# Down weights of expert 0 and up weights of expert 1 issued behind the load of the first expert's rows

## The reference

```
h = rms_norm(x)                                   # per token
group = argmax over 4 groups; top 2 of its 4 experts
a = h @ w1[e] ; b = h @ w3[e]                     # 16 experts, 1024 -> 256 each
hid = silu(a) * b * combine[e]
x = x + sum over the two experts of hid @ w2[e]   # 256 -> 1024
```

## Time and profile before

| | us |
|---|---|
| median of 3 runs | 1974.15 (1974.12 to 1975.18) |
| the profiled execution, its own time | 1973.74 |
| its span, first to last instruction | 1971.8 |
| matrix engine busy | 1899.3 (96%) |
| vector, scalar, GpSimd busy | 1134.3, 477.5, 400.4 |
| DMA moved | 376.32 MB, mean 191 GB/s |

### The profile page before, as it was taken

One profiled execution on the slowest core, in us unless ns is written; L12 is line 12 of the kernel. 1 busy time (PEld: TensorE's weight loads), 2 busy tenths in 40 slices (PEclk: granted clock), 3 DMA queues, 4 the chain that ended last, 5 costly groups with the idle time before them and its releaser, 6 DMA issues.

```text
span 1971.8 us, 25238 instructions
## 1 busy us (share of the span) xinstructions
PE 1899.3 (96%) x9028; PEld 1251.7 (63%) x9028; DVE 1134.3 (58%) x2171; ACT 477.5 (24%) x1048; POOL 400.4 (20%) x310
## 2 busy tenths in 40 slices
PE   8999999999999999999699999999999999999993
PEld 5655658755665545888565556586566655468882
DVE  4788732644786866111667886436457778641126
ACT  3133313343221011111132333132432300111112
POOL 1322233122220012000324222421222200210013
PEclk9999999999999999999899999999999999999997
DMA  4555677422328405999832121122223392179996
GB/s 178 203 203 203 228 276 270 176 99 79 127 86 322 156 33 217 411 393 369 329 112 113 75 75 75 43 86 81 86 86 118 126 347 91 70 274 424 384 373 235
DMA packets 77915, 376.32 MB, mean 191 GB/s; under 512 B 6705, under 2 KB 15281, under 8 KB 64578
## 3 DMA queue, kind: packets, MB, share of 16 engines
q1 hardware_dynamic: 43154, 260.35, 34.3%
q10 hardware_dynamic: 26000, 82.90, 11.0%
q0 software_dynamic: 8640, 31.46, 4.2%
HBM read 262.44 MB, written 113.30 MB: 191 GB/s over the span
## 4 chain that ended last, share of the span: by engine, by line
PE 89%; DVE 4%; DMA 3%; ACT 1%; issue 1%; POOL 1%; ACTq 0%; DVEq 0%; SPq 0%; POOLq 0%
PE bank L1030 41%; PE bank L2175 11%; PE bank L2035 8%; PE bank L2060 5%; PE bank L2210 5%; PE bank L1043 3%; PE bank L1056 2%; PE bank L1083 2%; PE bank L1121 2%; PE bank L742 2%; PE bank L1095 1%; PE bank L2167 1%; PE bank L1220 1%; PE bank L725 1%; DMA blocks<-ring,slots 1%
## 5 line engine op out<-in xcount | busy, mean ns | idle before, releaser
L1030 PE MATMUL bank<-x,ring 128*128 128x384 f32 x1056 | 360.2, 489 | 2.3 <-issue 2.3
L1030 PE MATMUL bank<-hT,ring 128*128 128x384 f32 x1056 | 359.7, 490 | 0.1
L1030 PEld LDWEIGHTS bank<-x,ring 128*128 128x128 f32 x1056 | 195.0, 190 | 135.2 <-issue 12.5
L1030 PEld LDWEIGHTS bank<-hT,ring 128*128 128x128 f32 x1056 | 195.3, 190 | 133.0 <-issue 10.2
L1525 DVE SCALAR_TENSOR_TENSOR reg_a<-cvx,pp,reg_a 128x783 f32<-128x783 f32 x120 | 142.7, 1189 | 4.3
L1284 ACT ACTIVATE sums<-bank 128x384 f32<-128x384 f32 x132 | 64.9, 491 | 250.0 <-PE bank L1030 243.9
L2571 DVE SCALAR_TENSOR_TENSOR prob<-prob,bank 128x256 f32<-128x256 f32 x30 | 12.6, 421 | 180.8 <-ACT prob L2290 180.7
L1468 DVE SCALAR_TENSOR_TENSOR gbuf<-bank,sums 128x384 f32<-128x384 f32 x96 | 53.5, 557 | 88.0 <-PE bank L1030 82.1
L1805 POOL TENSOR_TENSOR ring<-dg,ring 128x512 f32<-128x512 f32 x24 | 34.1, 1421 | 257.1 <-PE bank L1030 257.1
L2258 ACT ACTIVATE prob<-x 128x1024 f32<-128x1024 f32 x12 | 12.7, 1058 | 291.7 <-DVE x L2423 291.7
L2035 PE MATMUL bank<-oT,wide 128*128 128x384 f32 x256 | 82.9, 486 | 0.0
(11 more groups left out here) (387 smaller groups left out, 3276.2 us busy)
## 6 DMA issues: line engine op xcount, KB each, us to landing
ring<-in_wd SPq DMA_DIRECT2D x26, 2048.0 KB, 9.2
blocks<-hT SPq DMA_DIRECT2D x16, 3072.0 KB, 22.1
gate_dram<-gbuf ACTq DMA_DIRECT2D x64, 384.0 KB, 2.3
ring<-gate_dram SPq DMA_DIRECT2D x16, 1536.0 KB, 7.3
ring<-in_we SPq DMA_DIRECT2D x8, 2048.0 KB, 15.0
hT<-blocks ACTq DMA_DIRECT2D x26, 512.0 KB, 9.3
wide<-in_we SPq DMA_DIRECT2D x6, 2048.0 KB, 23.1
oT<-in_we SPq DMA_DIRECT2D x6, 2048.0 KB, 21.4
```

The lines of the kernel that those rows point to most:

```text
L1030: mm = nc.tensor.matmul(bank[i % 2][:, 0:HALF], w[:, k, :], a[:, k, :], start=(k == 0 and r in (0, 1, 3)), stop=(k == 3), skip_group_check ...
```

## The change

```
                 sp.wait_ge(out_mm, last_pair + 2)
                 load_up(sp, 0)
-                sp.wait_ge(out_mm, last_pair + 5)
-                load_down(sp, 0)
-                load_up(sp, 1)
                 sp.wait_ge(out_mm, last_pair + 6)
                 sp.wait_ge(scattered_first, 16 * TOP * FROM_BLOCKS * (layer + 1))
                 sp.dma_start(x_in[0], block_rows[0]).then_inc(block_in[0], 16)
+                load_down(sp, 0)
+                load_up(sp, 1)
                 sp.wait_ge(out_mm, last_pair + 7)
                 sp.wait_ge(scattered, 16 * TOP * (T - FROM_BLOCKS) * (layer + 1))
                 sp.wait_ge(block_in[1], 16)
```

## The result

| | before | changed |
|---|---|---|
| median of 9 runs, us | 1975.55 (1974.12 to 1977.14) | 1978.68 (1977.76 to 1982.62) |
| ratio, 95% interval | | 1.0018 (1.0009 to 1.0026) |
| span of the profiled execution, us | 1971.8 | 1976.5 |

A second timing of the changed kernel (`e4_after_again`, 11 runs) gave 1.0012 (1.0003 to 1.0021). So the change costs 0.12 to 0.18%, by these ratios 2.4 to 3.6 us. The change lies within the 0.2% that the prediction called no change, but it is measurable, and the predicted range (to 1978.0) does not reach the first median, 1978.68.

The account below looks back on a forecast made before the run. PE was taken as the bound, busy 1899.3 of 1971.8 us. Layer 0 -0.7 and layer 1 +1.6 gave +0.9 us, so 1974.6, plus 0.4 for the median: 1975.0; range 1971.4 to 1978.0.

Parts of the forecast that it names:

- the two weight loads held up the fourth tile's write: Ahead of the experts: SP's loads delayed GpSimd's write by 4.7 us in layer 0 and 3.7 us in layer 1.
- From the read to the end of the writes I had 17.8 us: Layer 0: block's read issued at 769.9, all tiles written (`scattered`) at 787.7, weights passing first, then the writes.
- In layer 1 I had +1.6 us: Layer 1: `scattered` at 1761.5 instead of 1759.89, so `turn_in(1)` at 1765.4 instead of 1763.74.
- the three signs that I had named for being wrong: ACT's rows issued before 786 or after 789.5; granted clock of 0.5 behind 791; PE waiting for expert 2's up weights.
- layer 0's term, -0.7 us: Layer 0: -0.2 us at `turn_in(1)` (791.3 against 791.51), and the 0.52 us wait for hidden values gone.
- With nothing of SP's in flight the write lands at 766.33 + 3.5.: Layer 0, fourth tile's write: landing at 769.85, 3.5 us as for the write at 746.67, instead of 8.2 us.
- the rows' own flight: Ahead of `turn_in(1)`: expert 1's rows take 3.56 us from ACT's issue, so PE can turn at 791.3.
- the collision itself: Tiles five and six: 3.15 MB of weights and 2.10 MB of writes pass together; `scattered` at 787.7, bounds 785.4 and 789.5.
- My own worst bound: All bytes at 324 GB/s, `scattered` at 789.5: layer 0 +1.0, layer 1 +3.4, together +4.4 us.
- the clock rival: Both layers: PE's idle 2.2 us ahead of `turn_in(1)` makes the clock fall, 1.7 us each; +4.3, 1978.4; chance 0.12.
- The rival "queues share": Tile five's writes go in between the weights, only tile six's are late; `scattered` near 785.5, time 1971.3; chance 0.16.
- its counter-evidence: Against sharing: from 764 to 768 GpSimd's queue had work (issued at 764.0 and 766.33) and moved nothing.

Follow-up runs that it names:

- e4_after_again: The changed kernel once more, unchanged, for a second profile and ratio; 1977.48 us, ratio to before 1.0012.
- e4: Short spelling of `e4_after_again`: the changed kernel once more, unchanged; 1977.48 us, ratio to before 1.0012.
- e8: The changed kernel with 34 (layer 0) and 17 (layer 1) idle transposes of the matrix engine ahead of `turn_in(1)`; ratio to before 1.0016.
- e2: Against the changed kernel: down weights of expert 0 back at their old place, up weights of expert 1 issued only when all tiles are written; 1981.81 us, 1.003.
- e3: Against the changed kernel: both moved weight loads issued only when all tiles are written; 1982.28 us, 1.0033.
- e6: The changed kernel's queue order and waits, with an eighth of the two moved loads' bytes (0.39 MB for 3.15 MB); 1971.22 us, 0.9978.
- e9: Against before: only the up weights of expert 1 (2 MB) moved behind the read of expert 0's block; 1971.24 us, 0.9978.
- before again: The kernel before, unchanged, for a second profile; its profiled execution took 1972.40 us.
- e1: Against before: only the down weights of expert 0 (1 MB) moved behind the read of expert 0's block; 1971.2 us, 0.9977.
- e7: Before with only the down weights of expert 0 (1 MB) moved behind the block's read, a repeat timing; 1971.9 us, 0.9978.

## Why the prediction was wrong

Right, by its own steps: the two weight loads held up the fourth tile's write; without them the block's read is issued 3.3 us (layer 0) and 3.7 us (layer 1) sooner; `turn_first` does not wait, and the one-hot matrix is next; the moved loads themselves are never late; the writes of tiles five and six pass behind the weights. From the read to the end of the writes I had 17.8 us; it was 17.9 and 17.6. In layer 1 I had +1.6 us, and it was +1.6, in part by luck: 1.3 at `turn_in(1)`, where 1.6 were forecast, and 0.3 behind it, where PE waits 0.44 us for expert 2's weights, which I had ruled out. Of the three signs that I had named for being wrong, two appeared, the granted clock at half behind 791 (0.52 from 794.1 to 797.4) and this wait; the third, rows issued after 789.5, appeared only on the profile's axis (789.65, or 789.25 without the 0.4 us by which the mark had moved).

Of the 3.7 us between the forecast 1975.0 and the median 1978.68, 1.4 are the base: I built on the first three runs of before (1974.15), and nine gave 1975.55. The rest is the change itself, +3.1 timed (+2.1 in `e4`) where I had +0.9; between the profiled executions the two layers show +4.3.

The step that failed is layer 0's term, -0.7 us; it measured +2.7. The 3.4 us are:
- **1.4 us, the write's landing.** "With nothing of SP's in flight the write lands at 766.33 + 3.5." In layer 0 it lands 4.9 us after its issue. The weights had held it up by 3.3 us (8.2 against 4.9), not by the 4.7 of the prediction. From the DMA issues of the changed kernel, that write in layer 0 and in layer 1:

```profile
blocks<-ring,slots POOLq DMA_INDIRECT x1, 4.9
...
blocks<-ring,slots POOLq DMA_INDIRECT x1, 3.5
```

and two queues of the same kernel from 765 to 770:

```profile
q0 software_dynamic: 278, 1.02, 50.8%
q8 instruction: 1, 0.02, 1.8%
```

A 16 KB packet of instructions (q8) passes there, and in layer 1 none does. One execution had it in layer 1 as well, `e8`, where the write took 5.4 us (its DMA from 1741 to 1746, and the issue at 1742):

```profile
q8 instruction: 1, 0.02, 2.3%
...
blocks<-ring,slots POOLq DMA_INDIRECT x1, 5.4
```

In the ten profiles of kernels with the read ahead of a moved load, this write took 4.9 to 5.4 us in the eleven places with such a packet, 3.5 in the seven without it and without SP's weights in flight, 4.2 in the two with weights. Both profiles of before had the packet in layer 0 too, and none in layer 1: the 8.2 against 7.2 us, which I had put down to the weights alone, may be in part this. That the packet causes the delay was not tested, and a packet during the flight is not enough: in seven profiles (`e2`, `e3`, `e6` to `e9` and before again) one passed in the last half microsecond of the write issued near 738, and this write took 3.5 us. In the changed kernel's late write it passed in the first half microsecond. I took my price from a write 20 us earlier.
- **0.4 us, the rows' own flight**, 3.98 us where I had 3.6.
- **1.4 us, the clock.** From `turn_in(1)` to `up(2)` it took 14.07 us instead of 12.71. This was a rival with a chance of 0.12. It was priced well (1.7 us), but placed in both layers and judged for an idle time of 2.2 us, from two waits of before: the granted clock was 0.50 behind the 1.64 us and 1.00 behind the 1.05 us (1751.2 to 1755). A limit read from these two did not hold: behind 2.00 us in layer 1 the clock stayed at 1.00 (1768.6 to 1773), behind 3.98 us in layer 0 it was 0.52. That its total, 1978.4, lies next to the median 1978.68 is luck. The first two errors made the idle time 3.98 us, where no wait up to 2.12 us had brought a fall. The full clock that the forecast took for `add_rows` was there, 2.05 us at 1.00 (779.3 to 781.3), where the forecast had 2.0.
- 0.1 us, the collision itself, and 0.1 of rounding.

The range was too narrow above. My own worst bound, +4.4 instead of +0.9, makes 1978.5, and the range stopped at 1978.0. In my own sum layer 0's slack was used up (ready at 789.05, rows at 791.3), so that each further us of delay was PE's, and I had bounded only one delay, the collision; for the landing I took one row where writes of the same kind alone took 3.4 to 5.7 us in the trace of before, and the clock rival, 1978.4, I left outside. The rival "queues share" failed too: GpSimd's queue got a fifth of the bytes only at the weights' very end. But its counter-evidence, the empty stretch from 764 to 768, was weaker than I read it: in the changed kernel the like write, issued at 764.40 with nothing of SP's in flight, moved its first packets no sooner than 766.9, so 2.5 us of that stretch are the write's own start.

What stays open: the timed medians of before (1975.09 to 1975.59) lie 1.4 to 3.2 us above its two profiled executions (1973.74 and 1972.40), so the spans of single profiles (1971.8 and 1970.5 against 1971.6, 1970.0 and 1970.7 for `e1`, `e7`, `e9`) show next to nothing of the 4 us that the timing has between them, and where before loses these in its median execution is not shown. At the place itself more can be seen: from the mark to `up(2)`, both layers together, before took 108.3 and 107.9 us, `e7` 105.8, `e9` 105.7, `e6` 105.7, and `e1`, with its clock falls, 108.1; the changed kernel took 112.6 and 112.3.

## What to carry to other kernels

Moving a transfer does not take its bytes away: ask who else needs the DMA engines in the stretch it moves to, and how much slack that user has. Here three places were tried for the same 3.15 MB, and each had its own victim (the first tiles' writes, the last tiles' writes, the next expert's rows); splitting the load between the first two places, 1 MB on one side of the read and 2 MB on the other, either way round, beat the better whole placement (before) by 0.22%. Splitting alone is not the recipe: `e2` splits too, with the 2 MB behind all writes, and is among the slowest. Where the sum ends next to a point at which slack turns into a wait, errors on one side are free and on the other are not: widen the range on that side.

## What the runs showed of the hardware

- While SP's weight loads were in flight, GpSimd's writes of 4 KB rows were held back nearly wholly: from 777 to 780 SP's queue moved 88 packets and 1.25 MB, GpSimd's none, of which only the first 0.4 us fall to the write's own start (1.5 us, as in `e6`). Beside 2 MB of weights (`e2`), expert 1's rows of 512 KB took 9.3 us instead of 3.56.
- One 16 KB packet of instructions near the start of an indirect write's flight went along with 1.4 to 1.9 us more for its landing (3.5 to 4.9 and 5.4 us); in the last half microsecond of the flight it went along with none (3.5 us). Cause not tested.
- With PE's waits ahead of `turn_in(1)`, which follow 7 us and more of unbroken products, the granted clock fell to 0.50 in the five cases of 2.54 us and more and stayed at 1.00 in the nine up to 2.12 us; a fall cost 1.4 us in layer 0 of the changed kernel, both times.
